# Token-tile seams around the dense layer, an earlier transposition of the first head, and a last expert weighted by halves

## What is computed

```python
for i in range(DEPTH):
    mod = c_act @ ada_w + ada_b
    sh1, sc1, g1, sh2, sc2, g2 = jnp.split(mod, 6, axis=-1)
    h = modulate(rmsnorm(x, n1), sh1, sc1)
    m = retention_mixer(h, *mix_p, row, col) if i == 0 else gqa_mixer(h, *mix_p, row, col)
    x = x + g1[:, None, :] * m
    h = modulate(rmsnorm(x, n2), sh2, sc2)
    f = swiglu(h, *ffn_p) if i == 0 else moe_swiglu(h, *ffn_p)
    x = x + g2[:, None, :] * f
return modulate(rmsnorm(x, final_norm_g), fsh, fsc)
```

## Time and profile before

| what | value |
|---|---|
| median of 3 runs | 1603.73 us (1601.40 to 1605.53) |
| the profiled execution | 1602.58 us |
| its span (first to last instruction) | 1600.5 us |
| mean granted TensorE clock, share of full speed | 0.983 |
| busy: PE, DVE, ACT, POOL | 1532.4, 1335.8, 980.6, 203.0 us |

### The profile page before, as it was taken

The page is one execution under the profiler, slowest core; times in us unless marked ns, Lnnn a source line. Parts: engine busy times, 40 slices in busy tenths (PEclk is TensorE's granted clock), DMA queues, the critical chain, the costliest instruction groups (busy, mean ns, idle before and its releaser), DMA issues.

```text
span 1600.5 us, 20512 instructions
## 1 busy us (share of the span) xinstructions
PE 1532.4 (96%) x6814; PEld 1229.2 (77%) x6814; DVE 1335.8 (83%) x1060; ACT 980.6 (61%) x803; POOL 203.0 (13%) x188
## 2 busy tenths in 40 slices
PE   6999997999989799999999999999999999999996
PEld 6777676777767588778888888888888888888784
DVE  6799779777777669998888988988988987988897
ACT  4554433443445555677777777767777777776773
POOL 0499700000020011001001001001000000000600
PEclk9999999999999999999999999999999999999998
DMA  9989727888884159999999999999999999999992
GB/s 342 379 285 354 259 82 247 288 295 297 274 293 145 39 211 337 385 346 371 376 359 370 376 359 368 379 360 369 376 358 369 381 352 363 384 356 368 383 366 106
DMA packets 238894, 508.67 MB, mean 318 GB/s; under 512 B 15494, under 2 KB 38150, under 8 KB 238728
## 3 DMA queue, kind: packets, MB, share of 16 engines
q1 hardware_dynamic: 233824, 491.52, 85.0%
q0 software_dynamic: 4448, 14.55, 2.5%
q10 hardware_dynamic: 584, 2.11, 0.3%
HBM read 502.12 MB, written 7.87 MB: 319 GB/s over the span
## 4 chain that ended last, share of the span: by engine, by line
PE 75%; DVE 11%; POOL 7%; issue 3%; ACT 2%; DMA 2%; SPq 0%; DVEq 0%; ACTq 0%; POOLq 0%
PE bank L1851 23%; PE bank L1853 23%; PE bank L1852 23%; DVE lo L1600 2%; PE bank L2242 1%; POOL proj L606 1%; POOL proj L605 1%; POOL ropet L602 1%; POOL ropet L601 1%; DVE hs L1255 1%; POOL ropet L603 1%; POOL proj L604 1%; DVE lo L1175 1%; PE bank L1954 1%; DVE ada_acc L1187 1%
## 5 line engine op out<-in xcount | busy, mean ns | idle before, releaser
L1600 DVE TENSOR_TENSOR lo<-stage,hi 128x2048 fp32r<-128x2048 f32 x168 | 385.6, 2302 | 46.2 <-ACT hi L1036 45.8
L1036 ACT CAST hi<-stage 128x2048 fp32r<-128x2048 f32 x168 | 321.3, 1914 | 114.7 <-DMA stage<-in_l_moe_w_up 92.6
L1852 PE MATMUL bank<-lo,hg_hi 128*128 128x512 f32 x896 | 353.3, 394 | 0.0
L721 ACT CAST hi<-stage 128x2048 fp32r<-128x2048 f32 x71 | 135.5, 1912 | 125.3 <-PE bank L1853 109.3
L1852 PEld LDWEIGHTS bank<-lo,hg_hi 128*128 128x128 f32 x896 | 168.5, 188 | 37.2
L1600 DVE TENSOR_TENSOR lo<-stage,hi_h 128x2048 fp32r<-128x2048 f32 x56 | 130.5, 2330 | 65.0 <-ACT hi_h L1036 65.0
L1175 DVE TENSOR_TENSOR lo<-stage,hi 128x2048 fp32r<-128x2048 f32 x71 | 163.3, 2304 | 25.5 <-ACT hi L721 19.0
L1853 PE MATMUL bank<-hi,hg_lo 128*128 128x512 f32 x452 | 178.7, 395 | 0.0
L1851 PE MATMUL bank<-hi,hg_hi 128*128 128x512 f32 x452 | 178.5, 395 | 0.2 <-issue 0.2
L1852 PE MATMUL bank<-lo,eaT_hi 128*128 128x512 f32 x448 | 177.2, 395 | 0.0
L1851 PE MATMUL bank<-hi,hT_hi 128*128 128x512 f32 x416 | 170.5, 410 | 2.4 <-DVE lo L1175 1.3
(11 more groups left out here) (329 smaller groups left out, 2772.0 us busy)
## 6 DMA issues: line engine op xcount, KB each, us to landing
stage<-in_l_moe_w_gate SPq DMA_DIRECT2D x224, 512.0 KB, 4.8
stage<-in_l_moe_w_up SPq DMA_DIRECT2D x224, 512.0 KB, 5.2
stage<-in_l_moe_w_down SPq DMA_DIRECT2D x224, 512.0 KB, 4.8
ada_w<-in_l_ada_w SPq DMA_DIRECT2D x40, 1024.0 KB, 5.2
stage<-in_l_ret_w_in SPq DMA_DIRECT2D x48, 512.0 KB, 6.9
stage<-in_l_ffn_w_gate SPq DMA_DIRECT2D x22, 512.0 KB, 7.7
stage<-in_l_ffn_w_up SPq DMA_DIRECT2D x22, 512.0 KB, 8.7
stage<-in_l_ffn_w_down SPq DMA_DIRECT2D x22, 512.0 KB, 6.6
```

Source lines behind the costliest of these rows:

```text
L721: nc.scalar.copy(hi[:, b % HRING, :], stage[:, b % RING, :]).then_inc(hi_done, 1)
L1036: nc.scalar.copy(hi_e(b), stage[:, b % RING, :]).then_inc(hi_done, 1)
L1600: nc.vector.tensor_tensor(lo[:, b % RING, :], stage[:, b % RING, :], hi_e(b).bitcast(F32), ALU.subtract).then_inc(lo_done, 1)
L1852: mm(dst_ap, a_hi, w_lo, start=False, stop=False)
```

## The change

- **First head.** `turn_first` is called inside the last projection unit, between its two token tiles, and no more ahead of that unit.
- **Seam into the dense layer.** `high` and `low` of the unit U_FF + 1 come ahead of the seam (its high part has a buffer of its own, `hi_f`; the one of U_QKV + 1 is `hi_q`). The residual, scale, squares, shift, transposition and first product go by token tile, most of them by halves of 512 columns. fin(6) moves behind the seam, fin(7) behind the next three units.
- **Seam out of it.** The last activation is transposed in the middle of the product of the one before, with buffers `faT2`; the residual, norm, transposition and the first two QKV units go by token tile. The last adaLN chunk of that pair (A_AT - 1) goes to the attention, in eight single steps among the heads, and `scale(3)` behind them.
- **Reading back.** GpSimd's four reads of the experts' rows go out one at a time, each when six more units have been used, and a tile's rows are added when its two are there.
- **Tail.** The routing weight of each of the last expert's rows is made by one more small matmul (`ix`). The product of the last expert is weighted (`weigh_down`) before the split, by halves, and after the scatter only added (`add_down`).

```diff
+        def hi_of(b):
+if b == U_FF + 1:
+    return hi_f[:, :]
+return hi_q[:, :] if b == U_QKV + 1 else hi[:, b % HRING, :]
...
 load_pair(U_FF, 0, slice(0, FCH))
+load_pair(U_FF + 1, 4, slice(0, FCH))
 load_fin(6)
-load_pair(U_FF + 1, 4, slice(0, FCH))
 load_fin(7)
...
-    if k in (2, 3):
-        load_ada(A_AT, k - 2, l1_ada_w, l1_ada_b, (A_AT - A_L1) * AC)
...
 load_gate_up(0, U_MOE, slice(0, ECH), 0)
+for half in range(2):
+    load_ada(A_AT, half, l1_ada_w, l1_ada_b, (A_AT - A_L1) * AC)
...
 pool.wait_ge(scale_done, 5)
+m = pool.value_load(meta[0:1, 2 * N_TAB + 1:2 * N_TAB + 2], min_val=0, max_val=3) * UNITS_ITEM
 for t in range(TT):
-    pool.dma_start(moe[:, t, :], yv[0, :, t, :]).then_inc(y_in, 16)
-    pool.dma_start(ysec[t][:, :], yv[1, :, t, :]).then_inc(y_in, 16)
-pool.wait_ge(y_in, 64)
-for t in range(TT):
+    for r, dst_ap in enumerate((moe[:, t, :], ysec[t][:, :])):
+        pool.wait_ge(w_used, m + (RING + U_END - 36 + 6 * (2 * t + r)))
+        pool.sem_inc(y_go, 1)
+        pool.dma_start(dst_ap, yv[r, :, t, :]).then_inc(y_in, 16)
+    pool.wait_ge(y_in, 32 * t + 32)
...
 high(U_FF)
+high(U_FF + 1)
 fin_take(1)
-high(U_FF + 1)
...
-norm(1, (3, 4))
-high_T(1)
+def half_square(t, n):
+    act.wait_ge(resid, 1 + t + 2 * n)
+    cols = slice(n * CB, (n + 1) * CB)
+    link(nc.scalar.activation(halfsq[:, :], xs[:, t, cols], ACT.Square, accum_out=gstat[:, t, n:n + 1]))
...
+for t in range(TT):
+    half_square(t, 0)
+    link(nc.scalar.activation(gstat[:, 4 + t, 0:1], gstat[:, t, 0:1], ACT.Identity, scale=1.0 / D, bias=eps))
+for t in range(TT):
+    half_square(t, 1)
+    nc.scalar.activation(root[:, t:t + 1], gstat[:, t, 1:2], ACT.Sqrt, scale=1.0 / D,
+                         bias=gstat[:, 4 + t, 0:1]).then_inc(root_done, 1)
+    high_T(1, (t,))
...
+high(U_QKV - 1)
...
-high(U_QKV - 1)
-ada_take(A_AT - 1, mod_at((A_AT - 1 - A_L1) * AC))
-f_high_act(N_FF - 1)
 high(U_QKV)
+f_high_act(N_FF - 1, faT2_hi)
 high(U_QKV + 1)
-norm(2, (6, 8))
-high_T(2)
+norm(2, (6, 8), (0,))
+high_T(2, (0,))
+norm(2, (6, 8), (1,))
+high_T(2, (1,))
...
+    if h == AH - 1:
+        ada_take(A_AT - 1, mod_at((A_AT - 1 - A_L1) * AC))
...
-    act.wait_ge(w_used, used)
-    nc.scalar.copy(dn_hi[:, :], bank[:, 4:6, :].rearrange("p b n -> p (b n)")).then_inc(dn_hi_done, 1)
+def take_down(n):
+    act.wait_ge(dn_w, n + 1)
+    cols = slice(n * CB, (n + 1) * CB)
+    nc.scalar.copy(dn_hi[:, cols], dnw[n][:, :]).then_inc(dn_hi_done, 1)
...
+nc.scalar.copy(ix[:, 30:31], bank[:, 3, SEQ:SEQ + 1])
...
 low(U_ROUT + 6)
-fin(6)
 low(U_ROUT + 7)
-residual(0, [(0, 0, bank[:, 0, :]), (0, 1, bank[:, 1, :])], [U_FF - 1] * 2)
 scale(1, A_IN)
 low(U_FF)
-residual(0, [(1, 0, bank[:, 6, :]), (1, 1, bank[:, 7, :])], [None, U_FF])
-norm(1, (3, 4))
-low_T(1)
 low(U_FF + 1)
-ada(A_FIN + 3, 1)
...
+def seam_residual(s, t, n, src):
+    m = mods[:, s % 2, 2]
+    cols = slice(n * CB, (n + 1) * CB)
+    link(nc.vector.tensor_tensor(hs[:, t, cols], src, m[:, cols], ALU.mult))
+    nc.vector.tensor_tensor(xs[:, t, cols], xs[:, t, cols], hs[:, t, cols], ALU.add).then_inc(resid, 1)
...
+def seam_shift(s, t):
+    dve.wait_ge(root_done, 2 * s + t + 1)
+    link(nc.vector.reciprocal(rstd[:, t:t + 1], root[:, t:t + 1]))
+    for n in range(2):
+        cols = slice(n * CB, (n + 1) * CB)
+        nc.vector.scalar_tensor_tensor(out=hs[:, t, cols], in0=hs[:, t, cols], scalar=rstd[:, t:t + 1],
+                                       in1=mods[:, s % 2, 0, cols], op0=ALU.mult,
+                                       op1=ALU.add).then_inc((h_half, h_ready)[n], 1)
...
+def out_scale(t, n):
+    dve.wait_ge(scale_done, 2)
+    dve.wait_ge(resid, 1 + t + 2 * n)
+    cols = slice(n * CB, (n + 1) * CB)
+    link(nc.vector.tensor_tensor(hs[:, t, cols], xs[:, t, cols], mods[:, 1, 1, cols], ALU.mult))
...
+for n in range(2):
+    for t in range(TT):
+        if n and t == 0:
+            dve.wait_ge(t0_done, 1)
+        else:
+            dve.wait_ge(w_used, RING + U_FF + n - 1)
+        seam_residual(0, t, n, bank[:, 6 * n + t, :])
+        out_scale(t, n)
+        if n:
+            seam_shift(1, t)
+            low_T(1, (t,))
+fin(6)
...
+f_units(0, 0)
+fin(7)
+for half in range(2):
+    ada(A_FF, half)
+f_units(0, 1)
+for half in range(2):
+    ada(A_FF + 1, half)
+last = (N_FF - 1) // 2 - 1
+with dve.Fori(1, last) as it:
     f_pair(it)
+f_units(last, 0)
+for half in range(2):
+    ada(A_AT - 2, half)
+f_units(last, 1)
+scale(2, A_L1 + 4)
+low(U_QKV - 1)
 f_mul(N_FF - 1)
-low(U_QKV - 1)
-f_low_act(N_FF - 1)
-scale(2, A_AT)
 low(U_QKV)
-residual(1, [(0, 0, bank[:, 4, :]), (1, 0, bank[:, 5, :]), (0, 1, bank[:, 6, :]), (1, 1, bank[:, 7, :])],
-         [None] * 2 + [U_QKV] * 2)
...
+for t in range(TT):
+    for n in range(2):
+        if t and n:
+            dve.wait_ge(w_used, RING + U_QKV)
+        else:
+            dve.wait_ge(t0_done, 2 + 2 * t + n)
+        seam_residual(1, t, n, bank[:, 4 + 2 * t + n, :])
+    seam_scale(2, t, 6 + 2 * t)
+    seam_shift(2, t)
+    low_T(2, (t,))
 low(U_QKV + 2)
 low(U_QKV + 3)
...
+ada_step(A_AT - 1, 0)
...
-scale(3, A_AT)
...
+def weigh_down(n):
+    dve.wait_ge(dn_part, n + 1)
+    cols = slice(n * CB, (n + 1) * CB)
+    nc.vector.scalar_tensor_tensor(out=dnw[n][:, :], in0=bank[:, 4 + n, :], scalar=ix[:, 30:31],
+                                   in1=mods[:, 1, 2, cols], op0=ALU.mult, op1=ALU.mult).then_inc(dn_w, 1)
...
+def low_down(n):
+    dve.wait_ge(dn_hi_done, n + 1)
+    cols = slice(n * CB, (n + 1) * CB)
+    nc.vector.tensor_tensor(dn_lo[:, cols], dnw[n][:, :], dn_hi[:, cols].bitcast(F32),
+                            ALU.subtract).then_inc(dn_done, 1)
...
-    if t == TT - 1:
-        low_down()
...
-last = dve.value_load(meta[0:1, bass.ds(passes - 1, 1)], min_val=0, max_val=E - 1)
-for t in range(TT):
-    dve.wait_ge(scat, t + 1)
-    link(nc.vector.scalar_tensor_tensor(out=hs[:, t, :],
-                                        in0=bank[:, (6, 4)[t]:(8, 6)[t], :].rearrange("p b n -> p (b n)"),
-                                        scalar=comb[:, t, bass.ds(last, 1)], in1=m,
-                                        op0=ALU.mult, op1=ALU.mult))
-    nc.vector.tensor_tensor(xs[:, t, :], xs[:, t, :], hs[:, t, :], ALU.add).then_inc(resid, 2)
-norm(4, (14, 16))
+dve.wait_ge(put_done, extra + (E + 1))
+def add_down(i):
+    n, t = i // 2, i % 2
+    cols = slice(n * CB, (n + 1) * CB)
+    dve.wait_ge(scat, i + 1)
+    nc.vector.tensor_tensor(xs[:, t, cols], xs[:, t, cols], bank[:, (6, 4)[t] + n, :], ALU.add).then_inc(resid, 1)
+weigh_down(0)
+low_down(0)
+weigh_down(1)
+add_down(0)
+low_down(1)
+for i in range(1, 4):
+    add_down(i)
+norm(4, (15, 16))
...
-            kg == 0, kg == 1, each=h0_done if u in (0, 3) else None, between=sum_second if u == 2 else None)
+            kg == 0, kg == 1, each=h0_done if u in (0, 3) else None,
+            between={2: sum_second, 2 * N_IN - 1: turn_first}.get(u))
...
-    if u == 2 * N_IN - 2:
-        pe.wait_ge(rope_done, 1)
-        turn_qk(0, 7, 0)
...
+        if t and between is not None:
+            between()
...
+for t in range(TT):
+    turn(1, (t,), 0)
+    for j in range(2):
+        h, l = unit(U_FF + j, 4)
+        pe.wait_ge(hT_done, 4 * 1 + 2 * t + j + 1)
+        tok = slice(t * P, (t + 1) * P)
+        for k in range(4):
+            ins = three(bank[:, t, :], hT_hi[:, 4 * j + k, tok], hT_lo[:, 4 * j + k, tok], h[:, k, :], l[:, k, :],
+                        j == 0 and k == 0, j == 1 and k == 3)
+        if t:
+            ins.then_inc(w_used, 1)
 f_turn(0)
...
+f_gate_up(U_FF + 2, 0, 1)
+ada_sum(A_FIN + 3)
+f_down(U_FF + 4, 0, 0, True, False)
+ada_sum(A_FF)
+f_turn(1)
...
+f_chunk(U_QKV - 7, 0, N_FF - 2, False, A_AT - 2)
+f_gate_up(U_QKV - 4, 0, N_FF - 1)
+f_down(U_QKV - 2, 0, N_FF - 2, False, False, between=lambda: f_turn(N_FF - 1))
+f_down(U_QKV - 1, 0, N_FF - 1, False, True, lhs=(faT2_hi, faT2_lo))
...
+for t in range(TT):
+    turn(2, (t,), 2)
+    for k in range(2):
+        pe.wait_ge(hT_done, 4 * 2 + 2 * t + k + 1)
+        qkv_half(k, t)
...
+        pe.wait_ge(aq_out, 5)
+        ada_sum(A_AT - 1)
...
+    for t in range(TT):
+        ins = mm(bank[:, 3, SEQ:SEQ + 1], pick[:, t, :].bitcast(F32), tokv[:, t, 9:10], start=(t == 0), stop=(t == TT - 1))
...
+def e_down_last(b, more, n):
+    pe.wait_ge(e_lo, n + 1)
+    parts = [unit_e(b + g, 2, more) for g in range(2)]
+    for c2 in range(2):
+        cols = slice(c2 * CB, (c2 + 1) * CB)
+        for k in range(4):
+            h, l = parts[k // 2]
+            ins = three(bank[:, 4 + c2, :], eaT2_hi[:, k, :], eaT2_lo[:, k, :], h[:, k % 2, cols], l[:, k % 2, cols],
+                        False, k == 3)
+        ins.then_inc(dn_part, 1)
...
+    for n in range(2):
+        pe.wait_ge(dn_done, n + 1)
+        cols = slice(n * CB, (n + 1) * CB)
+        for t in range(TT):
             mm(bank[:, (6, 4)[t] + n, :], put[:, t * P:(t + 1) * P], dn_hi[:, cols], start=True, stop=False)
```

(2 more changed lines are left out.)

162 lines of the change are left out of this document (90 added, 72 removed).

## The result

The changed kernel takes 1589.18 us (median of 4 runs, 1587.8 to 1589.74) against 1602.62 for the kernel before beside it: a ratio of 0.9911, with a 95% interval of 0.9896 to 0.9926. The forecast was 1587.5, in a range of 1582 to 1595. The profiled execution has a span of 1587.9 us, 12.6 less than before.

A forecast was written before the change was run, and what follows sets the result against it. TensorE's work lies end to end in the expert loop, so gains must come from its holes and the tail. Terms summed to -16.2 us, taking the profiled 1602.58 to 1586.4, as a median 1587.5; range 1582 to 1595.

The forecast's parts named there:

- First head, -4.2: Last projection unit: its tile 0 fills TensorE's idle time before the first head's transpositions; 4.2 us gained, bounds 2.9 to 4.4.
- Seam in, the tile-wise part, -2.0: Into the dense layer: work by token tile starts the first activation's transposition at 283.7, not 285.73; 2.0 us gained.
- What is given back, +4.4: Second dense activation: late fin(7) holds SyncE's queue, weights come late, TensorE stands 4.1 us; 4.4 us lost.
- The whole seam: Into the dense layer, tile-wise gain and late weights together: 2.4 us lost, bounds +2.0 to -4.5.
- Seam out, -5.8: Out of the dense layer: early last transposition and tile-wise work gain 5.8 us, after 1.2 off for low clock.
- Ada steps in the attention, -0.6: Attention heads: eight steps fit VectorE's gaps, scale(3) moves back; 0.6 us gained, up to +3 if gaps don't cover.
- Reads, -2.8: Late expert loop: fetching second rows one by one stops weights coming late; 2.8 us gained, bounds 0 to 3.1.
- Tail, -5.2: Kernel's end: weighting by halves before the scatter lets VectorE end sooner; 5.2 us gained, bounds 4.0 to 6.0.
- the weights coming in time: Rival at the seam in: dense weights land sooner or VectorE reaches fin(7) sooner; -20.6, 1583.1 us, chance 0.15.
- the late queue: Rival in the dense layer: SyncE's queue doesn't recover, eight following chunks each lose 4.1 us; 1620 us, chance 0.03.
- the one with both seams at their lower end: Rival: seams give only their lower ends, reads near 0; about -9.1, 1594.6 us, chance 0.17.

The follow-up runs named there:

- the second trace: The changed kernel itself run once more with no edit, beside the other kernels: 1587.85 us, ratio 0.9907.
- the first experiment: Against the changed kernel, VectorE's fin(6) moved into its 3.78 us gap at the seam in and fin(7) to fin(6)'s old place: 1583.62 us, ratio 0.9879.

## Why the prediction was right, step by step

- **First head, -4.2:** measured -3.98 in the profile of after and -3.5 to -3.8 alone. Right; the transpositions cost 1.09, where 1.0 was taken.
- **Seam in, the tile-wise part, -2.0:** measured -1.13. The transposition came at 262.0, which is 266.0 in the clock of before, not 265.1, and the first activation waited 1.41 us for the silu's end and the product, where I had 0.6 + 0.7 and hand-overs without a gap. Within the bounds (0 to 3.5), but too large by 0.9; the second trace has only 0.1, another execution with the same code 2.7.
- **What is given back, +4.4:** measured +4.29 at the second activation, by the mechanism named: fin(7) done at 289.8 (293.2 - 4.0 = 289.2 was predicted), queue, weights, hole of 3.26 (4.1 was predicted). The step that was missing is the clock behind the hole, +2.65 in this execution, 0 to 2.8 in others. I had charged TensorE's low clock at the seams and not here. The whole seam lost 5.8 us instead of 2.4 (5.8 in the second trace too) and left the bound that I had given (4.5).
- **Seam out, -5.8:** measured -7.28. The 1.2 us taken off for the low clock was the error: before had the same low clock behind its own wait of 7.45 us. Other executions of the same code gave between 5.0 and 7.3 (6.0 in the changed kernel's second trace), so 5.8 lies within their spread.
- **Ada steps in the attention, -0.6:** measured -0.28 from the attention's start to the first expert, but the same code gave between -2.8 (the changed kernel's own second trace) and +2.5 there in other executions, and the kernels with before's attention between -2.7 and +0.4. TensorE's waits for `prob` are 7.4 us instead of 7.0. The steps cost nothing that can be seen; that they gain 0.6 isn't shown, and no kernel undoes them alone.
- **Reads, -2.8:** measured -4.00, more than the bound of 3.1. I had counted the windows' missing busy time; a matmul behind a wait also starts its neighbours later (gaps of 0.45 to 0.62 us that count as busy), and the interval between transpositions, 20.85 and 17.90 us against 17.2, holds all of it.
- **Tail, -5.2:** measured -4.7, with +1.3 ahead of it that I had not priced: the small matmul 0.55, and the 0.7 whose cause is open. Net -3.4.
- The parts sum to -12.6 in the profile against -16.2 (with +0.5 in the expert loop ahead of the reads, which differs by as much between executions). Two terms were too good, the seam in by 3.4 and the tail by 1.8; two were too small, the seam out by 1.5 and the reads by 1.2. That these cancel in part is luck. The median, 1589.2, is nearer still, 1.7 from the forecast, since the profiled execution was the slowest of its four. Sign and range held, and so did the mechanism of each main term. Of the rivals, the weights coming in time fell (1583.1 would have been its time, and the first experiment, which makes them come in time, took 1583.6); the late queue didn't recur, the pace is 18.09 from the third activation on; the one with both seams at their lower end was half right, for the seam in alone.

## What to carry to other kernels

When a piece of work is moved later, follow what it releases: a buffer given back some 11 us later held a queue, and the queue's next entries were the weights for the engine that sets the time. Look for a gap of the engine that is at least as long as the piece, here VectorE's 3.78 us, and put it there. A hole in the busiest engine is worth closing only up to the next place where another engine is later; read that engine's waits up to there first.

## What the runs showed of the hardware

- The price of the low clock behind a wait isn't set by the code. The same matmuls behind a wait of 3.2 to 3.5 us took from 18.15 to 20.87 us in seven executions of the same instructions. The mean granted clock was 1.00 where they took 18.15, 0.91 for 19.72 and 0.87 for 20.74. A gain or loss under 3 us in a single execution has to be laid against that.
- Four reads of 0.5 MB together, beside weights that need 362 GB/s, made TensorE lose 3.4 us more than the same reads 11 to 17 us apart, which moved 395 to 398 GB/s in those chunks and cost nearly nothing.
- VectorE's low part (2.29 us, two inputs) waits out GpSimd's addition (2.59 us, two inputs) when it starts behind it: 4.49 and 4.50 us in two traces. Beside GpSimd's operations with one input it took 2.3 to 3.1.
